# State-space stage of a ten-stage block: reordered projection, decays by matmul and by exp's bias, heads in pairs, norm per chunk

## The chip, the cores and the metric

The kernel runs on one NeuronCore of a Trainium2 chip, in one launch. The metric is the device time of that launch in microseconds. The kernel before took 2258.63 us, the median of three runs (2258.62 to 2260.26).

## The reference, cut to what matters

Two blocks of layers are computed one after the other on x of 256 tokens by 1024, in float32: ten sublayers in all. The change touches the sixth, a bidirectional state-space mixer (Mamba-2 form) with 32 heads of 64 in 8 groups with a state of 128:

```python
z, xBC, dt = split(h @ w_in)            # 2048, 4096 and 2 x 32 columns
xBC = silu(centred_conv5(xBC) + bias)   # x: 2048, B: 8 x 128, C: 8 x 128
dt  = softplus(dt + dt_bias)            # for each direction d and head
a   = cumsum(dt * -exp(a_log))          # over tokens; from the end for the backward direction
# for each head and direction:
y[t] = sum over u (u <= t, or u >= t)  exp(a[t] - a[u]) * (C[t] . B[u]) * dt[u] * x[u]
y   = (y_forward + y_backward + d_skip * x) * silu(z)
y   = rms_norm(y, over each group of 256 channels) * norm_g
out = x_res + gate * (y @ w_out)        # w_out: 2048 x 1024
```

With 256 tokens the kernel computes each head's whole 256 by 256 matrix of decays, instead of chunks with a carried state. A head's matrix has four blocks of 128 by 128 tokens. The two on the diagonal are needed in both directions, each with a triangular mask, the other two in one direction: six blocks, 768 columns.

## The kernel before

Everything is written out as one list of instructions for each engine: PE (matmuls), ACT (activations), DVE (vector operations), and SP, which issues the DMAs. Each engine runs its list strictly in order. What one engine makes and another needs is ordered by semaphore counts (`wait_ge`); nothing else plans the work, so where a helper is called decides where its instructions stand in all four queues. `vl(...)` and `al(...)` count an instruction and wait for it on its own engine.

Weights come through a ring of four slots, three chunks (1.5 MB) a DMA. Matmuls with weights use three passes in the rounded format F32R: weight and operand are each split in a high part (a copy on ACT, L559) and a low part (a subtraction on DVE, L565). `split_chunk` does that for a chunk of 128 x 1024. Matmuls on plain float32 are shown in the trace as two records each, with two passes in each.

The stage goes as follows.

- `projection` (`main`, L622 for the first two chunks together, L652 for the rest, L646 for chunks computed by tokens). For each chunk c: split chunk c+1, 24 matmuls for chunk c, then `evac(c-1)`. Chunks 0 to 15 are z, 16 to 47 the convolution's channels, 48 is dt.
- `evac` (L2169): z gets its silu (L2175). A convolution chunk is copied to a padded tile (L2187), scaled by the first tap on ACT (L2189), gets four more taps on DVE (L2197), and its silu on ACT one chunk later (`silu_out`, L2226).
- Then a chain on small tiles: exp of -|dt|, a series for log1p (L2242 to L2252), dtA, cumulative sums as matmuls with triangles of ones (L2269, L2273), the gate row (`gate_row`, L539), transposes of x (L2294) and their copies (L2300).
- The loop over heads. `group(gi)`: once for 4 heads, the product of B and C (L2323), four copies into the order of the six blocks (L2332 to L2335), and four products of x and dt (L2346). `rows(h)`: two matmuls bring a[t] to all partitions (L2363). `decays(h)`: DVE forms a[t] - a[u] plus the mask in six operations (L2377, L2379, L2380), ACT makes one exp over 768 columns (L2386). `sums(h)`: DVE multiplies by the group's product (L2396), PE makes four matmuls (L2407 to L2410) of 64 output channels; odd heads write to the upper half of the partitions. `finish(h)`, every second head: the skip term and the product with silu(z) (L2426, L2428).
- The norm: squares of all 4096 columns (L2454), sums over channels with a matmul of ones (L2468), scale, root (L2480), reciprocal over 2048 columns (L2485), 16 products (L2487).
- `out_project`: for each of 16 chunks, split the operand (L693, L698), split the weights (L559, L565), 12 matmuls of 512 columns (L709).

Of the kernel before, what the change touches and what calls it, by code (L numbers as in the profile page):

```python
# [8 lines left out]
F32R = mybir.dt.float32r  # L9
# [5 lines left out]
P = 128  # L15
# [102 lines left out]
def lay_out(i):  # L118
# [39 lines left out]
    for j in range(5):  # L158
# [33 lines left out]
        "w_ssd_in": col_chunks(padded(i["ssd_w_in_2"][0], 49 * P)),  # L192
# [31 lines left out]
def build(nc, dram, out, pat, cat):  # L224
    V, A, E = nc.vector, nc.scalar, nc.tensor
    ctx = ExitStack()
    with ctx:
# [7 lines left out]
        hT_ = sb("hT", KC * T)  # L235
        htok_ = sb("htok", NT * D)
# [7 lines left out]
        sb("slab", SLAB // 4)  # L244
        psum = ctx.enter_context(nc.psum_tensor("psum", [P, 8, 512], F32))
# [419 lines left out]
        def out_project(name, n, lhs, ready, nxt, parts_at=R_AT + 24576, wp_at=(R_AT, R_AT + 8192, R_AT + 16384)):  # L665

            parts = halves(parts_at, 4)
            wp = [chunk_parts(at) for at in wp_at]
            wp_free = [ready] * 3
            parts_free = [ready] * 4  # L670
            loads, done = [], []
# [8 lines left out]
            for k in range(n):  # L680
# [6 lines left out]
                s, full = loads[k // 3]  # L687

                @block.scalar
                def _(_e):  # L690
                    for point in parts_free[k % 4]:
                        A.wait_ge(*point)
                    Ring.p = act.count(A.activation(parts[:, 0, k % 4, :], lhs[:, k, :], ACT.Copy).then_inc(act.sem, 1))  # L693
# [6 lines left out]
                w_ready = split_chunk(slot_ap(s, SLOT)[:, (k % 3) * D:(k % 3 + 1) * D], wp[k % 3], full, wp_free[k % 3])  # L700
                Ring.used[s] = [w_ready]

                @block.tensor
                def _(_e):
                    E.wait_ge(*w_ready)
# [1438 lines left out]
        def ssd_run(h_pts, project, nxt):  # L2144
            ar = Region(W_AT + 24576)
            bc = ar.take(16 * T).rearrange("p (c t) -> p c t", t=T)
            xb_ = ar.take(16 * T)
            xb = xb_.rearrange("p (c t) -> p c t", t=T)
            zs_ = ar.take(16 * T)
            zs = zs_.rearrange("p (c t) -> p c t", t=T)  # L2150
            dt, dtA, acum = (ar.take(NT * 64) for _ in range(3))
# [3 lines left out]
            ar = Region(H_AT, W_AT + 24576)  # L2155
            tmp = [ar.take(NT * 64) for _ in range(3)]
            acT = ar.take(T)
# [9 lines left out]
            cv_free = [go] * 2  # L2167

            def evac(c, b, p):  # L2169
                if c < 16:  # L2170
                    @block.scalar
                    def _(_e):
                        A.wait_ge(*p)
                        A.wait_ge(*pad_ready)
                        Ring.q = act.count(A.activation(zs[:, c, :], b[:, 0:T], ACT.Silu).then_inc(act.sem, 1))  # L2175
                    return (Ring.q,)
                if c < 48:
                    m = c - 16
                    q = m % 2

                    @block.scalar
                    def _(_e):

                        A.wait_ge(*p)
# [18 lines left out]
                    return (freed,)  # L2203
                while pend:
                    silu_out()

                @block.vector
                def _(_e):

                    V.wait_ge(*p)  # L2210
                    bias = prm("dt_bias")
                    bb = spread(bias.rearrange("p (o n) -> p o n", o=1), [P, NT, 64])
                    vl(V.tensor_tensor(d3(dt), d3(b[:, 0:2 * 64]), bb, ALU.add).then_inc(dve.sem, 1))
                    vl(V.tensor_scalar(tmp[0], dt, -1.0, None, ALU.mult).then_inc(dve.sem, 1))
                    Ring.q = vl(V.tensor_tensor(tmp[0], tmp[0], dt, ALU.min).then_inc(dve.sem, 1))
                return (Ring.q,)

            pend, cv_silu = [], [go] * 2

            def silu_out():  # L2220
                m, q, p = pend.pop(0)

                @block.scalar
                def _(_e):
                    A.wait_ge(*p)
                    cv_silu[q] = act.count(A.activation(xb[:, m, :] if m < 16 else bc[:, m - 16, :], cv[q], ACT.Silu, bias=prm("sconv_b")[:, m:m + 1]).then_inc(act.sem, 1))  # L2226

            project(evac, h_pts)
            xt = [hT_[:, :], htok_[:, :]]
            neg_abs = Ring.q  # L2230

            @block.scalar
            def _(_e):
                A.wait_ge(*neg_abs)
                A.activation(Arow, prm("a_log"), ACT.Exp)
                Ring.q = al(A.activation(tmp[0], tmp[0], ACT.Exp).then_inc(act.sem, 1))

            @block.vector
            def _(_e):

                V.wait_ge(*Ring.q)
                vl(V.tensor_scalar(tmp[1], tmp[0], 2.0, None, ALU.add).then_inc(dve.sem, 1))  # L2242
                vl(V.reciprocal(tmp[1], tmp[1]).then_inc(dve.sem, 1))
                vl(V.tensor_tensor(tmp[0], tmp[0], tmp[1], ALU.mult).then_inc(dve.sem, 1))
                vl(V.tensor_tensor(tmp[1], tmp[0], tmp[0], ALU.mult).then_inc(dve.sem, 1))
# [531 lines left out]
```

## Time and profile before

| | |
|---|---|
| median of the runs | 2258.63 us |
| the profiled execution's own time | 2257.68 us |
| its span | 2255.9 us |
| PE busy | 2008.1 us, 89% |
| DVE busy | 1518.6 us, 67% |
| ACT busy | 1160.3 us, 51% |
| POOL busy | 0.2 us |
| mean granted clock of PE | 0.937 of full |
| DMA | 377.90 MB, 168 GB/s |

PE is the TensorE's matmuls and PEld its weight loads, DVE the VectorE, ACT the ScalarE, POOL the GpSimd. Busy is the time in which an engine has at least one instruction under way. The granted clock is 1.00 at 2.4 GHz and 0.50 at 1.2 GHz. The span goes from the first to the last instruction of the program; what lies around it (1.8 us) is part of the execution's time. The stage that the change touches goes from about 1091 to 1466 us of the span.

### The profile page before, as it was taken

Reading aid. Unit: us, or ns where it says so; the run is one execution under the profiler, and the core shown is the slowest. Engines: PE = TensorE matmul, PEld = TensorE weight load, DVE = VectorE, ACT = ScalarE, POOL = GpSimd, SP = SyncE. Lnnn points to the kernel's source line nnn. Section 1 sums busy time; section 2 is a strip of 40 time slices with the busy share of each in tenths; the row PEclk is TensorE's granted clock in tenths of the full one; section 3 lists DMA queues with packets and bytes.
Section 4 is the critical chain, followed back from the end, with each engine's and each line's share of the span. In section 5 each row is a group of like instructions: output and inputs, shape, how many; then the busy total and the mean of one; then the engine's idle time right before and its main releaser. Section 6 shows DMA issues by size and latency. Waiting matters only on the chain.

```text
span 2255.9 us, 36817 instructions
## 1 busy us (share of the span) xinstructions
PE 2008.1 (89%) x14906; PEld 1805.3 (80%) x14906; DVE 1518.6 (67%) x2429; ACT 1160.3 (51%) x2013; POOL 0.2 (0%) x4
## 2 busy tenths in 40 slices
PE   7896999898788998999999785799999997689998
PEld 6895999897568997999898553689989995368998
DVE  5667877523757777877578796687777772466554
ACT  6535665532546566665566332465565652355342
POOL 0000000000000000000000000000000000000000
PEclk9998999995889999999999898899999997789999
DMA  7203765433026664888343100468858860304551
GB/s 291 100 4 131 262 232 187 158 124 120 1 82 225 219 231 165 315 291 284 141 156 135 57 1 1 162 249 283 286 208 311 283 242 24 130 2 167 190 176 74
DMA packets 96538, 377.90 MB, mean 168 GB/s; under 512 B 5745, under 2 KB 5873, under 8 KB 95601
## 3 DMA queue, kind: packets, MB, share of 16 engines
q1 hardware_dynamic: 96368, 375.54, 46.9%
q8 instruction: 119, 1.95, 0.3%
q14 instruction: 51, 0.41, 0.1%
HBM read 374.47 MB, written 1.05 MB: 166 GB/s over the span
## 4 chain that ended last, share of the span: by engine, by line
PE 76%; DVE 18%; ACT 3%; issue 2%; DMA 0%; DVEq 0%; SPq 0%; ACTq 0%
PE psum L902 32%; PE psum L918 15%; PE psum L652 7%; PE psum L709 5%; DVE htok L2197 3%; PE psum L646 2%; DVE buf L565 2%; PE psum L1152 2%; PE psum L885 2%; PE psum L2616 1%; PE psum L494 1%; PE psum L2070 1%; DVE buf L2396 1%; PE psum L1520 1%; DVE buf L2377 1%
## 5 line engine op out<-in xcount | busy, mean ns | idle before, releaser
L902 PEld LDWEIGHTS psum<-buf,buf 128*128 128x128 f32 x6048 | 741.9, 192 | 9.3
L902 PE MATMUL psum<-buf,buf 128*128 128x256 f32 x6048 | 745.7, 283 | 0.0
L918 PE MATMUL psum<-buf,buf 128*128 128x512 f32 x1584 | 383.5, 391 | 2.2 <-DVE buf L967 2.2
L918 PEld LDWEIGHTS psum<-buf,buf 128*128 128x128 f32 x1584 | 289.2, 188 | 57.8 <-DVE buf L967 3.0
L800 DVE TENSOR_TENSOR buf<-ring,buf 128x1024 fp32r<-128x1024 f32 x264 | 311.1, 1220 | 9.5 <-DVE modT L856 7.5
L652 PE MATMUL psum<-buf,buf 128*128 128x256 f32 x2064 | 256.7, 285 | 9.2 <-DVE buf L565 9.1
L794 ACT ACTIVATE buf<-ring 128x1024 fp32r<-128x1024 f32 x264 | 263.0, 1045 | 0.0
L652 PEld LDWEIGHTS psum<-buf,buf 128*128 128x128 f32 x2064 | 249.7, 192 | 15.2 <-DVE buf L565 14.6
L565 DVE TENSOR_TENSOR buf<-ring,buf 128x1024 fp32r<-128x1024 f32 x132 | 161.2, 1224 | 129.2 <-ACT buf L559 120.3
L816 DVE TENSOR_TENSOR buf<-ring,buf 128x1024 fp32r<-128x1024 f32 x132 | 161.6, 1224 | 86.4 <-ACT buf L811 86.4
L811 ACT ACTIVATE buf<-ring 128x1024 fp32r<-128x1024 f32 x132 | 139.5, 1057 | 87.9 <-PE psum L918 85.3
L829 DVE TENSOR_TENSOR buf<-buf,crow 128x1024 f32<-128x1024 f32 x144 | 171.8, 1218 | 0.0
L559 ACT ACTIVATE buf<-ring 128x1024 fp32r<-128x1024 f32 x132 | 138.1, 1049 | 43.7 <-PE psum L709 34.4
L936 ACT ACTIVATE htok<-psum 128x256 f32<-128x256 f32 x88 | 33.8, 384 | 229.1 <-PE psum L902 229.1
L709 PE MATMUL psum<-buf,buf 128*128 128x512 f32 x480 | 118.0, 410 | 37.4 <-DVE buf L565 37.4
L840 ACT ACTIVATE buf<-buf 128x1024 f32<-128x1024 f32 x144 | 150.8, 1052 | 0.0
L963 DVE TENSOR_TENSOR htok<-htok,psum 128x256 f32<-128x256 f32 x132 | 55.3, 419 | 135.6 <-ACT htok L936 129.8
L709 PEld LDWEIGHTS psum<-buf,buf 128*128 128x128 f32 x480 | 95.7, 200 | 59.3 <-DVE buf L565 38.7
L494 PE MATMUL psum<-early,htok 128*128 128x128 f32 x160 | 41.5, 427 | 69.8 <-DVE htok L483 69.1
L494 PEld LDWEIGHTS psum<-early,htok 128*128 128x128 f32 x160 | 27.6, 203 | 84.0 <-DVE htok L483 76.7
L948 DVE SCALAR_TENSOR_TENSOR htok<-htok,params 128x256 f32<-128x256 f32 x88 | 42.7, 485 | 57.7 <-ACT htok L942 56.2
L2197 DVE SCALAR_TENSOR_TENSOR htok<-htok,params 128x256 f32<-128x256 f32 x128 | 61.9, 484 | 5.1 <-ACT htok L2189 1.3
(339 smaller groups left out, 2116.9 us busy)
## 6 DMA issues: line engine op xcount, KB each, us to landing
ring<-in_w_ffn SPq DMA_DIRECT2D x88, 1536.0 KB, 7.1
buf<-in_w_mod SPq DMA_DIRECT2D x144, 512.0 KB, 4.7
ring<-in_w_conv SPq DMA_DIRECT2D x44, 1536.0 KB, 6.6
ring<-in_w_ssd_in SPq DMA_DIRECT2D x16, 1536.0 KB, 6.4
ring<-in_w_ns_in SPq DMA_DIRECT2D x9, 1536.0 KB, 6.3
ring<-in_w_hy_in SPq DMA_DIRECT2D x7, 1536.0 KB, 19.0
ring<-in_w_ssd_out SPq DMA_DIRECT2D x5, 1536.0 KB, 6.4
ring<-in_w_cmp SPq DMA_DIRECT2D x4, 1024.0 KB, 4.8
```

Source lines behind the costliest of these rows:

```text
L559: Ring.p = act.count(A.activation(parts[:, 0, :], raw, ACT.Copy).then_inc(act.sem, 1))
L565: Ring.p = dve.count(V.tensor_tensor(parts[:, 1, :], raw, whole(parts[:, 0, :]), ALU.subtract).then_inc(dve.sem, 1))
L652: ins = E.matmul(b[:, 0:T], w[:, wa, k, :], h[:, ha, k, :], start=k + n_ == 0, stop=k == KC - 1 and n_ == 2)
L709: ins = E.matmul(acc[:, t, h * 512:(h + 1) * 512], parts[:, la, k % 4, t * P:(t + 1) * P], wp[k % 3][:, wa, h * 512:(h + 1) * 512], start= ...
L794: Ring.p = act.count(A.activation(wu[j % 2][:, 0, part], raw, ACT.Copy).then_inc(act.sem, 1))
L800: up_split[j, g] = dve.count(V.tensor_tensor(wu[j % 2][:, 1, part], raw, whole(wu[j % 2][:, 0, part]), ALU.subtract).then_inc(dve.sem, 1))
L811: Ring.p = act.count(A.activation(wd[j % 2][:, 0, :], raw, ACT.Copy).then_inc(act.sem, 1))
L816: down_split[j] = dve.count(V.tensor_tensor(wd[j % 2][:, 1, :], raw, whole(wd[j % 2][:, 0, :]), ALU.subtract).then_inc(dve.sem, 1))
L829: mod_prod[c] = dve.count(V.tensor_tensor(w, w, crow[:, :], ALU.mult).then_inc(dve.sem, 1))
L840: Ring.mod_last = act.count(A.activation(w, w, ACT.Copy, accum_out=modT[:, c:c + 1]).then_inc(act.sem, 1))
L902: ins = E.matmul(b[:, g * T:(g + 1) * T], w[:, wa, g, k, :], h[:, ha, k, :], start=k + n_ == 0, stop=k == KC - 1 and n_ == 2)
L918: ins = E.matmul(acc[:, t, g * 512:(g + 1) * 512], hr[z][:, ha, t * P:(t + 1) * P], wd[z][:, wa, g * 512:(g + 1) * 512], start=j == 0 and ...
```

## The change

The stage is rewritten from the projection to the output projection. The input weights are laid out in another order: two convolution chunks and one z chunk in turn, B and C ahead of x, and dt as chunk 2. The chain for dt, the cumulative sums, the transposes of x and the gate row are issued in `evac`, beside the projection's chunks (`beside(c)`). dt no longer multiplies x: its logarithm goes, with -a[u], into the bias of exp. The argument of exp is summed in PSUM by PE: the mask through an identity, a[t] (as high and low part, on 64 partitions) through a selection vector, both in F32R; ACT reads it from there in four operations of 256, 256, 128 and 128 columns. Sums and finish go by pairs of heads, with the two heads' matmuls in turn. The squares are made in `finish`, their sums on PE with one column, and the norm's factors are brought back to all partitions by 16 matmuls; the products with them are issued chunk by chunk inside `out_project` (`feed`). The first chunk group of the output weights is loaded behind the projection, and two of its chunks are split inside the loop. Some tiles move (acT, idr, sel into the unused end of htok; dt, bias, u1 into `small`).

```diff
+def ssd_order():
+    conv = [c for g in range(8) for c in (32 + g, 40 + g)] + list(range(16, 32))
+    out = conv[0:2] + [48]
+    for j in range(1, 14):
+        out += conv[2 * j:2 * j + 2] + [j - 1]
+    return out + conv[28:32] + [13, 14, 15]
...
-            load_a, load_b, pre_a, pre_b, project = projection("w_ssd_in", 49, h, tokens=(48,), widths={48: 64})
+            load_a, load_b, pre_a, pre_b, project = projection("w_ssd_in", 49, h, tokens=(2,), widths={2: 64})
...
+            def turn_x(n):
+                for t in range(NT):
+                        # PE
+                        E.wait_ge(*x_made[4 * n + 3])
+                        E.wait_ge(*at["t_free", t])
+                        for c in range(4):
+                            ins = E.transpose(bank(t)[:, c * P:(c + 1) * P], xb[:, 4 * n + c, t * P:(t + 1) * P], ident)
+                        # ACT
+                        at["t_free", t] = act.count(A.activation(xt[t][:, 4 * n * P:(4 * n + 4) * P], bank(t), ACT.Copy)...)
+            def beside(c):   # called at the end of evac(c)
+                if c == 3:   # DVE: waits for exp; u1 = bias + 2, reciprocal, bias *= u1, u2 = bias^2, u3 = u2 / 17
+                if c == 4:   # DVE: horner((15, 13, 11, 9)), one operation a term
+                if c == 5:   # DVE: horner((7, 5, 3)), then three operations for dt
+                if c == 6:   # DVE: dtA (4 operations), bias = max(dt, 1e-37)
+                        A.wait_ge(*at["floor"])
+                        at["log"] = al(A.activation(u1, bias, ACT.Ln).then_inc(act.sem, 1))
+                        at["back"] = act.count(A.activation(u2, u1, ACT.Exp, scale=-1.0).then_inc(act.sem, 1))
+                if c == 7:   # PE: waits for dtA; 6 matmuls of 64 columns into bank(0). DVE: two operations on u2, u1
+                if c == 8:   # DVE: waits for them; acum = bank(0), bias = u1 - acum
+                if c == 9:   # PE: 4 transposes of acum; ACT: acT = their high part
+                if c == 10:  # DVE: low part of acT, idr = ident, sel = ident[:, 0:32] + ident[:, 32:64]
+                if c == 12:
+                    at["row"] = gate_row(mod_col(0, 1, 2), 1.0, 2, [h_pts[-1]])
+                if c in (31, 37, 43, 47):
+                    turn_x((31, 37, 43, 47).index(c))
...
+            def group(gi):   # PE: two matmuls; ACT: waits for them and, from gi = 2, for g_used[gi - 2]
+                    A.activation(G_[q][:, 0:512], bank(4), ACT.Copy)
+                    ends = bank(4).rearrange("p (a n) -> p a n", a=4)[:, 0:4:3, :]
+                    g_made[gi] = act.count(A.activation(G_[q][:, 512:768]..., ends, ACT.Copy)...)
+            def rows(h):     # PE: waits for x_free[h - 2]
+                    E.matmul(X[q][:, 0:512], idr, masks[:, 0:512], start=True, stop=False)
+                    E.matmul(X[q][:, 0:512], one_head, acT[0:64, :], start=False, stop=True)
+                    E.matmul(X[q][:, 512:768], idr, masks[:, 384:640], start=True, stop=False)
+                    ins = E.matmul(X[q][:, 512:768], one_head, acT[0:64, 128:384], start=False, stop=True)
+            def exponentials(h):
+                    A.wait_ge(*at["X", h])
+                    if h >= 4:
+                        A.wait_ge(*y_summed[(h - 4) // 2])
+                    A.activation(two_of(0), x4[:, 0:4:2, :], ACT.Exp, bias=by(0, 0))
+                    A.activation(two_of(256), x4[:, 1:4:2, :], ACT.Exp, bias=by(1, 1))
+                    A.activation(e[:, 512:640], X[h % 2][:, 512:640], ACT.Exp, bias=by(0, 1))
+                    x_free[h] = act.count(A.activation(e[:, 640:768], X[h % 2][:, 640:768], ACT.Exp, bias=by(1, 0))...)
+            def products(h): # DVE: waits for x_free[h] and g_made; e *= G, 768 columns
+            def sums(c):     # PE: waits for products(2c + 1), y_free[c - 2]
+                    for n, (u, lo, w, to) in enumerate(((0, 0, 256, 0), (0, 512, 128, 0), (1, 640, 128, 128), (1, 256, 256, 0))):
+                        for o in range(2):
+                            h = 2 * c + o
+                            ins = E.matmul(y[o * HD:(o + 1) * HD, to:to + w], xt[u][:, h * HD:(h + 1) * HD],
+                                           ee[h % 4][:, lo:lo + w], start=n == 0, stop=n == 3)
+            def finish(c):   # DVE: skip term, times silu(z), square
+            def square_sums(c): # PE: two matmuls of one column
+            load_table(ACT.Exp)
+            rows(0)
+            group(0)
+            rows(1)
+            for n in range(18):
+                if n < 16:
+                    exponentials(2 * n)
+                    exponentials(2 * n + 1)
+                if n < 15:
+                    rows(2 * n + 2)
+                if 1 <= n <= 16:
+                    sums(n - 1)
+                if n < 15:
+                    rows(2 * n + 3)
+                if n % 2 and n < 15:
+                    group(n // 2 + 1)
+                if n < 16:
+                    products(2 * n)
+                    products(2 * n + 1)
+                if n >= 2:
+                    square_sums(n - 2)
+                if 1 <= n <= 16:
+                    finish(n - 1)
+                if n == 12:
+                    split_out(0, [projected])
+                if n == 14:
+                    split_out(1, [y_free[7]])
+            load_table(ACT.Sqrt)
+            # DVE: waits for the last square sums, reduce to 16 values, scale; ACT: root; DVE: reciprocal
+                for gi in range(8):   # PE
+                    for t in range(NT):
+                        ins = E.matmul(bank(4 + gi // 2)[:, gi % 2 * T + t * P:gi % 2 * T + (t + 1) * P],
+                                       spread(rs[:, 8 * t + gi:8 * t + gi + 1], [P, P]), ident, start=True, stop=True)
+            def feed(k):     # called in out_project ahead of chunk k; DVE: x times gain times factor, chunks k and k + 1
+                norm(k)
+                norm(k + 1)
+                return normed[k]
```

## Rows read from the trace of the kernel before

**Rows 1.** Windows: stretch, length; busy PE, PEld, DVE, ACT, POOL; granted clock, DMA share, GB/s.
```profile
1091.80:1249.70 157.90, 148.74 (x1185) 143.26 (x1183) 117.39 (x183) 92.37 (x161) 0.00 (x0) 1.00 0.40 144
1249.70:1271.40 21.70, 14.16 (x79) 11.77 (x77) 9.23 (x32) 7.38 (x13) 0.00 (x0) 0.69 0.22 73
1271.40:1381.40 110.00, 89.05 (x413) 56.82 (x412) 101.46 (x284) 34.88 (x64) 0.00 (x0) 1.00 0.00 1
1381.40:1421.20 39.80, 8.74 (x32) 7.12 (x32) 24.31 (x24) 9.46 (x8) 0.00 (x0) 0.68 0.00 0
1421.20:1466.40 45.20, 45.17 (x188) 37.16 (x189) 27.91 (x37) 22.76 (x33) 0.00 (x0) 0.94 0.55 203
```

**Rows 2.** Timeline in the projection's z part: start, length, engine, line, tiles, count.
```profile
1136.81 11.44 PE L652 MATMUL psum<-buf,buf 128*128 128x256 f32 x94
```

**Rows 3.** Timeline in the projection's convolution part.
```profile
1161.80 1.23 DVE L565 TENSOR_TENSOR buf<-ring,buf 128x1024 fp32r<-128x1024 f32 x1 [0.30 <-DVE htok L2197]
1162.94 2.04 DVE L2197 SCALAR_TENSOR_TENSOR htok<-htok,params 128x256 f32<-128x256 f32 x4
1163.08 3.13 PE L652 MATMUL psum<-buf,buf 128*128 128x256 f32 x24 [0.34 <-DVE buf L565]
1166.56 3.14 PE L652 MATMUL psum<-buf,buf 128*128 128x256 f32 x24 [0.36 <-DVE buf L565]
```

**Rows 4.** PE groups by form: the dt chunk's matmuls.
```profile
L646 PE MATMUL psum<-ring,hT 128*128 128x64 f32 x32 | 3.7, 273 | 0.0
```

**Rows 5.** Timeline behind the projection: the chain for dt.
```profile
1250.20 1.28 ACT L2235 ACT_TABLE_LOAD   x1
1250.46 0.29 DVE L2215 TENSOR_TENSOR buf<-buf,buf 128x128 f32<-128x128 f32 x1
1251.50 0.26 ACT L2235 ACTIVATE buf<-params 128x64 f32<-128x64 f32 x1
1252.25 0.95 DVE L2243 RECIPROCAL buf<-buf 128x128 f32<-128x128 f32 x1
```

**Rows 6.** Group by line in the loop: count, busy, mean ns, idle before.
```profile
L2396 DVE TENSOR_TENSOR buf<-buf,buf 128x768 f32<-128x768 f32 x32 | 30.5, 952 | 0.3 <-DVE buf L2428 0.3
```

**Rows 7.** Timeline in the loop over heads.
```profile
1283.05 0.48 DVE L2426 SCALAR_TENSOR_TENSOR buf<-buf,params,psum 128x256 f32<-128x256 f32 x1
1283.56 0.42 DVE L2428 TENSOR_TENSOR buf<-buf,buf 128x256 f32<-128x256 f32 x1
1284.32 0.38 PE L2410 MATMUL psum<-buf,buf 128*64 128x128 f32 x2
1284.64 1.13 PE L2363 MATMUL psum<-buf,early 64*128 64x256 f32 x4
```

**Rows 8.** Two PE groups of the first stage that alternate between halves of the array.
```profile
66.56 1.97 PE L1338 MATMUL psum<-early,small 128*64 128x128 f32 x32
L1511 PE MATMUL psum<-buf,buf 64*64 64x64 f32 x128 | 3.8, 221 | 0.0
```

**Rows 9.** ACT timelines: two operations with a bias from PSUM; one without.
```profile
34.20 0.84 ACT L1255 ACTIVATE buf<-psum,params 128x256 f32<-128x256 f32 x2 [0.19 <-PE psum L1248]
...
1271.94 0.28 ACT L2334 ACTIVATE buf<-psum 128x128 f32<-128x128 f32 x1
```

**Rows 10.** Chain of waits after the stage: start, length, engine, line, count.
```profile
1483.14 1.78 PE psum L539 x16
1490.68 2.75 PE psum L918 x12
```

**Rows 11.** Timeline of the norm.
```profile
1382.39 3.62 ACT L2454 ACTIVATE buf<-buf 128x4096 f32<-128x4096 f32 x1 [4.68 <-DVE buf L2428]
1386.06 8.74 PE L2468 MATMUL psum<-buf,buf 128*128 128x256 f32 x32 [4.68 <-ACT buf L2454]
1399.11 12.95 DVE L2485 RECIPROCAL htok<-htok 128x2048 f32<-128x2048 f32 x1 [1.98 <-ACT htok L2480]
```

**Rows 12.** Window at the start of the output projection, columns as in rows 1.
```profile
1422.00:1426.00 4.00, 4.00 (x11) 3.12 (x10) 2.45 (x4) 0.73 (x2) 0.00 (x0) 0.50 0.22 35
```

More of the change, by code:

```diff
@@ new lines, in evac, with _ @@
+            def evac(c, b, p):
+                o = order[c]
+                if o < 16:
+                    while c > 45 and pend:
+                        silu_out()
+                    @block.scalar
+                    def _(_e):
+                        A.wait_ge(*p)
+                        Ring.q = act.count(A.activation(zs[:, o, :], b[:, 0:T], ACT.Silu).then_inc(act.sem, 1))
+                    freed = Ring.q
+                elif o < 48:
+                    m = o - 16
+                    q = len(x_made) + len(pend) & 1
@@ new lines, in evac, with split_out @@
+                beside(c)
+                return (freed,)
+            project(evac, h_pts)
+            projected = (pe.sem, pe.n)
+            z_made = (act.sem, act.n)
+            row_point = at["row"]
+            wp_at = (H_AT + 8192, R_AT + 24576, R_AT)
+            wp = [chunk_parts(a) for a in wp_at]
+            out_load = load(dram["w_ssd_out"][0:3], 3)
+            out_split = {}
+            def split_out(k, free):
+                s, full = out_load
+                out_split[k] = split_chunk(slot_ap(s, SLOT)[:, k * D:(k + 1) * D], wp[k], full, free)
+                Ring.used[s] = [out_split[k]]
@@ L2238, in _ @@
+            ar = Region(W_AT, W_AT + 24576)
+            masks = ar.take(5 * P, F32R)
+            G_ = [ar.take(768) for _ in range(2)]
+            ee = [ar.take(768) for _ in range(4)]
+            sq = [ar.take(T) for _ in range(2)]
+            rs = small[:, 192:208]
             @block.vector
             def _(_e):
-                V.wait_ge(*Ring.q)
-                vl(V.tensor_scalar(tmp[1], tmp[0], 2.0, None, ALU.add).then_inc(dve.sem, 1))
-                vl(V.reciprocal(tmp[1], tmp[1]).then_inc(dve.sem, 1))
@@ L2313, in group @@
+                V.memset(whole(masks[:, P:3 * P]), 0.0)
+                for a, name in ((0, "neg_f"), (3, "neg_b"), (4, "neg_f")):
+                    ins = V.tensor_copy(masks[:, a * P:(a + 1) * P], cst(name))
+                at["masks"] = dve.count(ins.then_inc(dve.sem, 1))
+            X = [banks(2 * q, 2) for q in range(2)]
+            x_free, e_free, e_made, m_made = {}, {}, {}, {}
+            g_made, g_used, y_summed, y_free, sq_made, sq_free = {}, {}, {}, {}, {}, {}
             def group(gi):
@@ L2430, in ssd_run @@
-            group(0)
-            rows(0)
-            for h in range(34):
-                if h + 1 < 32:
-                    rows(h + 1)
-                if h < 32:
-                    decays(h)
-                if h % 4 == 1 and h // 4 + 1 < 8:
-                    group(h // 4 + 1)
-                if 1 <= h <= 32:
-                    sums(h - 1)
-                if h >= 2:
-                    finish(h - 2)
-            y_done = [(dve.sem, dve.n), (pe.sem, pe.n)]
-            sq = zs_
-            inv = htok_[:, :]
```

444 lines of the change are left out of this document (218 added, 226 removed).

## Prediction

> **What bounds the kernel now.** I read the busy totals first, then five windows over the state-space stage, then their timelines. PE is busy 89% of the span, but not in this stage. [rows 1] cut it into projection (157.9 us), a chain for dt (21.7), the loop over 32 heads (110.0), the norm (39.8) and the output projection (45.2). The reader is to see which engine fills each: PE in the first and last; nobody in the second and fourth, at a granted clock of 0.69 and 0.68; DVE, 101.5 of 110, in the loop. The change touches the first four: 329.4 us from the first matmul (1091.8) to the first of the output projection (1421.2).
>
> Within the projection a z chunk costs its 24 matmuls, 24 x 0.12 = 2.88 us [rows 2]. A convolution chunk costs 3.48 from 1163.08 to 1166.56 [rows 3]: DVE's subtraction, four taps (2.04) and 0.3 of gaps, for which PE waits 0.34. So 16 chunks are bound by PE, 32 by DVE.
>
> **Projection.** The new order has two convolutions and one z in three chunks. DVE needs 2 x 3.48 + about 1.3 = 8.3 us, PE 3 x 2.88 = 8.64: PE is the bound, by a little. PE's floor is 6.0 for the first pair, 46 x 2.88 = 132.5, and 32 x 0.115 = 3.7 for dt [rows 4]: 142.2. Into it move six matmuls for the cumulative sums (12 records, 1.4), four transposes (0.5), the gate row (1.8, L539 in [rows 10]) and 24 of 32 transposes of x (2.6): 6.3. Before, the gate row lay under DVE's chain.
>
> The dt chain is no longer alone, but it stands in DVE's queue between taps and subtractions, and PE waits for subtractions. Counted from the end of chunks 0 and 1: DVE starts at 0.9, has six convolutions' taps (6 x 2.35 = 14.1), the subtractions of chunks 3 to 10 (8 x 1.23 = 9.8), 24 small operations at 0.32 (a 0.29 operation and its wait, [rows 5]) and 0.65 more for the reciprocal (8.3). It also stands still about 3.1 us while ACT makes Exp and, later, Ln and Exp, behind which ACT's copy of the next weights is queued. So chunk 10 starts at 36.3; with PE alone it would be 3.7 + 7 x 2.88 + 1.4 = 25.3. Loss 11.0. Later, transposes of x and the gate row make ACT wait for PE before its next copy: about 0.5 a time, four times, 1.9. Projection: 142.2 + 6.3 + 11.0 + 1.9 = 161.4, so 3.5 more than before. Bounds: 149 if queues absorb it all, 168 if the ACT stalls double. If DVE's 0.3 us of slack in three chunks is not there, the later 38 chunks add up to 4 of this.
>
> ACT switches tables Silu to Exp, to Silu, to Ln and Exp, to Silu here. The row shows a switch at 1.28, the next operation 0.02 after it, and the load under way at 1250.20, before DVE made its operation's input at 1250.46 to 1250.75 [rows 5]: it runs ahead of the wait; I count it only where ACT returns to Silu. The Trainium skill, "ScalarE: Activation LUTs", "What ACT_TABLE_LOAD costs", gives about 2.66 us a switch, of which 1.38 is a drain. By that figure four switches would add 5.5 us to the total; the trace here shows no drain, so I leave it out.
>
> **From the projection's end to a running loop.** 21.7 us of chain go. Late next is ACT's last silu and turn of x (2.1 us after the end), then rows(0), the first group's product and its copies (5.3), exponentials of heads 0 and 1 and rows(2), rows(3): the steady loop starts 9.2 after the end. DVE's masks (1 us) lie under this.
>
> **The loop.** Removed from DVE: six subtractions a head and the 32 products with dt (12 us). Its new work for two heads is two products of 0.95 and three finishing operations (0.48, 0.42, 0.42 and waits): 3.3 us [rows 6, 7]. ACT: an operation on 256 columns from PSUM with a bias is 0.47, the next starts 0.36 after it two take 0.84 [rows 9]; one on 128 without a bias is 0.28, with it I take 0.37, spacing 0.25. A head is 0.36 + 0.36 + 0.25 + 0.37 = 1.33 (bounds 1.2 and 1.6); two heads 2.5, and every second pair two copies for the group, 0.8.
>
> PE: one pass over 512 columns in the rounded format is 2.75/12 = 0.229, over 256 it is 0.12 [rows 10, 2]. Rows of a head are two of each, 0.70. A change between K=128 and K=64, or to M=64, costs 0.09: L2363 starts 0.20 after the last record of L2410, whose usual spacing is 0.11 [rows 7]. Four changes make rows 1.07. Sums: 768 columns in plain f32 took 1.28 us a head (4 x 768 / 2.4 GHz; spacing 0.11 for 128 columns bears that out). Interleaved, two heads write to different halves of the array. L1338 does just that, with one moving operand for both halves: its 32 records of 128 columns take 1.97, 0.055 each and not 0.11 [rows 8]. L1511 alternates halves with operands of their own: 128 records of 64 columns take 3.8, 0.03 each, where two passes over 64 columns are 0.053 [rows 8]. So two heads cost 1.28 + 0.1 = 1.4. A group's product is 0.95 (one in two pairs), square sums 0.53. A pair is 2 x 1.07 + 1.4 + 0.5 + 0.53 = 4.5: above ACT and DVE. PE becomes the bound.
>
> But the order of ACT's queue adds a wait. The group's copies stand ahead of the next pair's exponentials, and wait for a product that PE makes last in the iteration. Over two iterations, from a start a: rows 1.07, sums to 2.45, rows to 3.5, product 4.5 and 0.17 until it has landed, copies, exponentials from 5.5 to 6.85, rows (waiting since 5.1) to 7.95, sums to 9.35, landed 9.55, exponentials to 10.9, next start at 10.95. Two pairs take 10.95, not 9.0. Seven such cycles hold 14 pairs; the last sums end 9.2 + 6 x 10.95 + 14.4 = 89.3 after the projection's end. Splitting the first output weights (1.05 ACT, 1.23 DVE, twice) falls in even iterations, where ACT is done at 7.8 and waits until 9.55: hidden; without that cover 1 us each. Per head: 2.7 us against 3.44.
>
> **Norm.** Gone are the squares (3.6), the sums over 4096 columns (8.7), a root over 2048 columns, the reciprocal (12.95) and most of the 16 products [rows 11]. Left in line: finish 1.45, square sums 0.6, reduce and scale 0.5, root 0.4, reciprocal of 16 values 0.3, then PE's 16 broadcast matmuls, 32 x 0.11 = 3.5, ahead of the output projection in its queue. The first norm products and the split of x lie under these. 6.75, and 1.0 because PE has paused and may be granted half the clock for a part: 97.1 after the projection's end. The table load of Sqrt is hidden, as it is now. The remaining norm products (0.48 a chunk) join 1.65 of DVE in chunks of 2.75: hidden, until DVE is over 2.75.
>
> **Output projection.** Before, its first four microseconds ran at 0.50 [rows 12], after 18 us without a matmul. The pause is now below 4: I take 1.6 us off (0 to 2.4). Weight DMAs are issued well ahead as before, on SP, which waits for slots only; none is added.
>
> **Sum.** 161.4 + 97.1 = 258.5 for 329.4: 70.9 less, and 1.6: 72.5. The profiled execution took 2257.68 us (span 2255.9 and 1.8 around it), 1 us under the median of 2258.63. 2257.7 - 72.5 = 2185.2, so 2186 as a median.
>
> **Rivals.**
> - Loop runs at PE's 4.5 a pair, because ACT gets through sooner (or matmuls of K=64 and K=128 follow without 0.09): 7 x 2 less, 2172. For: ACT's rows leave no doubt that it is under 3.4 us a pair; against: its queue is in order. 15%.
> - The halves don't overlap: no row has two streams of 128 partitions and 256 columns at once (L1338 shares one, L1511's have 64 partitions). 1.28 more a pair, 20 in all, 2206. Against: both rows as far as they go. 8%.
> - A full drain at each change of form. The row has L2363 at 1284.64 while L2410 lasts until 1284.70, so there was none in this case [rows 7]. If there were, 0.07 more at 11 changes in 16 pairs is 12 us: 2198. The Trainium skill, "TensorEngine Tiling (Array Packing)", "Key Properties", says that a change of tiling mode drains the TensorE; the trace speaks against a whole drain. 7%.
> - The early projection is the bound: ACT's returns to Silu and DVE's small operations delay PE by 10 more. For: DVE has only 0.3 us to spare in three chunks, so that a delay is not worked off. 2196. 17%.
> - Slower: PE, which waits in every cycle, is granted half its clock from the loop on. PE's parts of a cycle double: 17.7 instead of 10.95, 47 more over the loop, 10 at its ends, and 41 in the output projection if the clock stays down through it: 2284. It decides once over 73 us come together, that is the whole loop and a third of the output projection at half clock. Against: now PE idles 20 us of the loop and has 1.00 [rows 1]. 3%.
>
> **How the numbers follow.** Forecast 50%, its own range 2178 to 2194. The range of 8 in 10 takes in the first rival and the second: 2166 to 2208. 0.2% (4.5 us) is what can be told from no change. Everything but the slow rival is faster: 95%; same 2%, slower 3%, a little more than its own case for mishaps.
>
> **What would show it.** Projection about 161 us with PE gaps in chunks 5 to 10 and hardly any afterwards; PE's first row of the loop 3 us behind it; L-lines of sums in pairs that start within 0.01 us; ACT waiting for the group's product, some 2 us every second pair; period 10 to 11 us; norm below 10 us; DVE below 70% in the loop. Wrong would be: sums spaced at 0.21, a granted clock below 0.95 in the loop, or a projection over 170.

## The result and the profile after

The changed kernel took 2234.30 us, the median of four runs (2232.84 to 2235.93); the kernel before took 2258.62 beside it. The ratio is 0.9893, with an interval from 0.9881 to 0.9905: 24 us faster, a third of the 72.5 forecast, and outside the range of 2166 to 2208. The profiled execution took 2232.84 us, its span is 2231.1 us.

The page of the kernel after, busy time:

```profile
PE 2023.7 (91%) x14962; PEld 1811.3 (81%) x14962; DVE 1452.3 (65%) x2226; ACT 1175.9 (53%) x2102; POOL 0.2 (0%) x4
```

PE is busy for 15.6 us longer than before although the kernel is faster, and DVE 66 us less. The windows of the stage after, with the columns of [rows 1]: projection, loop, norm, and the output projection with 1.3 us behind it.

```profile
1090.60:1256.40 165.80, 156.18 (x1244) 153.28 (x1243) 126.58 (x214) 104.78 (x179) 0.00 (x0) 0.97 0.42 149
1256.40:1390.40 134.00, 119.03 (x481) 68.41 (x479) 53.07 (x83) 54.87 (x153) 0.00 (x0) 0.69 0.02 9
1390.40:1397.10 6.70, 4.70 (x40) 4.54 (x41) 4.25 (x12) 1.60 (x5) 0.00 (x0) 1.00 0.00 0
1397.10:1440.90 43.80, 43.80 (x195) 35.94 (x193) 32.61 (x48) 22.23 (x32) 0.00 (x0) 1.00 0.59 210
```

The reader is to see the second line. The chain for dt [rows 1] is gone as a stretch of its own, and of the four that are left, the norm and the output projection came out about as forecast and the projection is 4.4 us too long. The loop, 134.0 us with its start, was forecast at 89.3. PE is busy 119 us of it, at a granted clock of 0.69; DVE and ACT are at 40%.

The chain of waits after, from the last sums (L2488) through the norm to the end of the output projection (L727):

```profile
1388.86 1.55 PE psum L2488 x16
...
1393.52 3.84 PE psum L2566 x32
1397.36 42.23 PE psum L727 x186
```

The whole norm takes 7.0 us where before it took 39.8, 12.95 of them in one reciprocal [rows 1, 11]. The last sums of the loop, at the full clock again, take 1.55.

From the first matmul of the projection to the end of the output projection the stage takes 349.0 us; the forecast has 302.1 (374.6 less 72.5). The 46.9 between them, in the forecast's own terms:

| | forecast | measured | difference |
|---|---|---|---|
| projection | 161.4 | 165.8 | +4.4 |
| end of the projection to the last sums | 89.3 | 134.0 | +44.7 |
| norm | 7.75 | 7.0 | -0.8 |
| output projection | 43.6 | 42.2 | -1.4 |

Outside the stage, its start is 1.2 earlier and what follows it is 2.0 longer, which the forecast left alone and no run looked into.

PE's timeline after, over one cycle of two pairs in the loop (rows L2438 to L2441, sums L2488, group product L2412):

```profile
1311.50 0.80 PE L2438 MATMUL psum<-buf,buf 128*128 128x512 f32 x1 [1.56 <-ACT buf L2461]
...
1313.97 1.55 PE L2488 MATMUL psum<-buf,hT 128*64 128x256 f32 x8
1315.30 1.49 PE L2488 MATMUL psum<-buf,buf 128*64 128x128 f32 x8
...
1318.66 0.48 PE L2438 MATMUL psum<-buf,buf 128*128 128x512 f32 x1
1319.07 0.49 PE L2439 MATMUL psum<-buf,buf 64*128 64x512 f32 x1
1319.49 0.39 PE L2440 MATMUL psum<-buf,buf 128*128 128x256 f32 x1
1319.81 0.38 PE L2441 MATMUL psum<-buf,buf 64*128 64x256 f32 x1
1320.12 1.55 PE L2488 MATMUL psum<-buf,hT 128*64 128x256 f32 x8
1321.46 1.49 PE L2488 MATMUL psum<-buf,buf 128*64 128x128 f32 x8
...
1324.65 1.13 PE L2412 MATMUL psum<-buf 128*128 128x256 f32 x4
...
1327.99 0.79 PE L2438 MATMUL psum<-buf,buf 128*128 128x512 f32 x1 [1.87 <-ACT buf L2461]
```

The cycle is 16.5 us, 1311.50 to 1327.99, where 10.95 was forecast. It is the shortest of six: from one wait to the next they take 16.5 to 18.0 us, 17.1 on average. There are two new things in it. First, a head's rows take 1.46 even at the full clock, 1318.66 to 1320.12, not 1.07. Second, most of the cycle isn't at the full clock. Windows of the same cycle:

```profile
1311.50:1314.00 2.50, 2.50 (x6) 1.18 (x6) 1.90 (x2) 1.20 (x4) 0.00 (x0) 0.50 0.00 0
1314.00:1316.70 2.70, 2.70 (x17) 1.58 (x16) 0.00 (x0) 0.00 (x0) 0.00 (x0) 0.50 0.00 0
1316.70:1318.60 1.90, 1.90 (x10) 1.15 (x8) 1.64 (x4) 1.66 (x5) 0.00 (x0) 1.00 0.00 0
...
1320.10:1322.90 2.80, 2.80 (x18) 1.64 (x17) 0.55 (x1) 0.00 (x0) 0.00 (x0) 0.50 0.00 0
```

The clock is at 1.2 GHz behind the wait, at 2.4 from 1316.7 (rows of a head at the full clock follow, 1318.66 on), and back at 1.2 at 1320.1, with no idle time on PE ahead of this second fall. The sums of a pair take 2.83 us at half clock. Why this one cycle goes back to the full clock between them, no run looked into.

ACT's timeline after shows the wait that the forecast had put into the cycle, its copy of the group's product:

```profile
1309.33 0.60 ACT L2421 ACTIVATE buf<-psum 128x512 f32<-128x512 f32 x1 [7.29 <-PE psum L2412]
```

### The profile page after: what moved, and what is told of

The parts are those of the page before. It is cut to its first block, busy times and chain, and to the rows that moved or that the text cites. A ratio compares the mean times of both kernels' runs of the same rounds, so it can differ in the third digit from the quotient of the medians.

```text
span 2231.1 us, 36837 instructions
## 1 busy us (share of the span) xinstructions
PE 2023.7 (91%) x14962; PEld 1811.3 (81%) x14962; DVE 1452.3 (65%) x2226; ACT 1175.9 (53%) x2102; POOL 0.2 (0%) x4
## 4 chain that ended last, share of the span: by engine, by line
PE 83%; DVE 11%; ACT 4%; issue 2%; DMA 0%; DVEq 0%; SPq 0%; ACTq 0%
PE psum L920 32%; PE psum L936 15%; PE psum L662 9%; PE psum L727 5%; PE psum L656 2%; PE psum L2488 2%; PE psum L1170 2%; PE psum L903 2%; PE psum L2713 1%; PE psum L504 1%; PE psum L2088 1%; DVE buf L575 1%; PE psum L1538 1%; PE psum L1143 1%; DVE buf L1089 1%
## 5 line engine op out<-in xcount | busy, mean ns | idle before, releaser
L727 PE MATMUL psum<-buf,buf 128*128 128x512 f32 x480 | 115.4, 403 | 11.4 <-DVE buf L575 11.4
L727 PEld LDWEIGHTS psum<-buf,buf 128*128 128x128 f32 x480 | 93.8, 196 | 32.2 <-DVE buf L575 12.2
```

Source lines behind the costliest of these rows:

```text
L727: ins = E.matmul(acc[:, t, h * 512:(h + 1) * 512], parts[:, la, k % 4, t * P:(t + 1) * P], wp[k % 3][:, wa, h * 512:(h + 1) * 512], start= ...
```

## The experiments

All kernels do the whole computation. The theories of the first four runs: (A) PE falls to half clock because its matmuls fill too little of the loop's time; (B) the pairwise sums, alternating between the array's halves, lower the clock by their form; (C) the wait for ACT alone does it. From e5 on there are two more, about the time of a head's rows: (D) changes between operands of 128 and 64 partitions (K=128 and K=64) cost more than forecast; (E) the cost lies elsewhere. A loop time below is that of its window, from the projection's end to the last sums, in a profiled run. The kernel before had medians of 2259.11, 2259.99 and 2259.76 us beside the three sets (e1 to e4, e5 to e8, e9 to e11).

### e1: the sums head by head

```diff
-                    for n, (u, lo, w, to) in enumerate(...):
-                        for o in range(2):
+                    for o in range(2):
+                        for n, (u, lo, w, to) in enumerate(...):
```

> The changed kernel, but the sums of a pair run head by head (the loop over heads outside the loop over blocks), so that its matmuls no longer alternate between the halves of the array. Theory A (share: the clock is halved because the array streams for too small a share of the loop, since interleaving halves the time of the sums and the waits for ACT stay): streaming goes up by 1.3 us a pair, the granted clock of the loop from 0.68 to 0.95 or more, sums of a pair again about 2.7 us, a cycle of two pairs 13.6 instead of 16.5, about 2216 us. Theory B (form: matmuls in halves are not counted as activity): also 0.95 or more and about 2216. Theory C (the wait for the group's copies alone makes the clock fall): that wait is still there, the clock stays near 0.68, the sums take up to 5 us, 2250 or more.

Measured: 2238.19 us, ratio 0.9906 (0.9891 to 0.9920). Window of its loop:

```profile
1257.90:1393.90 136.00, 120.57 (x482) 77.46 (x480) 53.05 (x83) 54.75 (x153) 0.00 (x0) 0.81 0.02 10
```

The sums get longer, the loop stays about as long, and the clock is higher, 0.81 and not 0.69, but not full. None of the three theories had this: A and B had 0.95 or more and 2216 us, C had 0.68 and 2250 or more. Pairing does not slow the kernel, but whether it lowers the clock this run can't say: longer sums also fill PE's time otherwise.

### e2: the group's product at the head of the iteration

```diff
             for n in range(18):
+                if n % 2 and n < 15:
+                    group(n // 2 + 1)
                 if n < 16:
...
-                if n % 2 and n < 15:
-                    group(n // 2 + 1)
```

> The changed kernel, but PE makes the group's product at the head of the iteration, ahead of rows(2n+2), instead of at its end, so that ACT does not wait for it ahead of the next exponentials. [...] Theory B (form): the clock stays near 0.68, PE is busy nearly all the time at half clock, 2225 to 2235. Theory C (the wait alone): 1.00, about 2182.

Measured: 2205.45 us, ratio 0.9765 (0.9751 to 0.9780). Window of its loop:

```profile
1256.90:1360.70 103.80, 101.39 (x481) 59.27 (x480) 53.15 (x83) 56.29 (x153) 0.00 (x0) 0.82 0.03 13
```

The wait is gone: PE idles 2.4 us of the loop, not 15. That accounts for 12.6 of the 30.2 us; the rest is in the busy time, which goes with the clock of 0.82. So the time is not B's (2225 or more), and without the wait the clock is still not full, so C is not the whole of it. The clock also moves inside this loop: its window from 1297 to 1317 has 1.00, with cycles of 10.6 us, and the one from 1337 to 1360 has 0.61, though PE idles only 0.4 us in it.

### e3: eight matmuls more in every pair

```diff
+                    for _i in range(8):
+                        E.matmul(bank(7)[:, 256:512], idr, masks[:, 0:256], start=True, stop=True)
...
+                if n < 16:
+                    fill()
```

> The changed kernel with eight more matmuls of 256 columns in the rounded format (idr times masks into an unused part of bank 7, read by nobody) behind each pair's square sums, where PE waits for ACT: 0.86 us more of work a pair at full clock. Theory A (share): the granted clock of the loop rises to 0.95 or more, although the work is more, a cycle of two pairs falls from 16.5 to about 12, 2200 to 2208. Theory B (form): the windows of the sums stay at half clock; 2232 to 2255, the filler costs or is hidden. Theory C (the wait alone, which the filler covers): as A.

Measured: 2217.73 us, ratio 0.9817 (0.9802 to 0.9831): 16.6 us faster than the kernel after, by work that nobody reads. Window of its loop, and its timeline at a pair's sums (L2488) beside the added matmuls (L2519):

```profile
1257.90:1373.50 115.60, 107.98 (x609) 70.54 (x607) 53.15 (x83) 54.75 (x153) 0.00 (x0) 0.94 0.03 11
```

```profile
1313.66 1.19 PE L2519 MATMUL psum<-buf,buf 128*128 128x256 f32 x8
...
1316.07 0.87 PE L2488 MATMUL psum<-buf,hT 128*64 128x256 f32 x8
1316.77 0.82 PE L2488 MATMUL psum<-buf,buf 128*64 128x128 f32 x8
```

128 matmuls more, and PE is busy 11 us less. The clock is about what A had, the time is 10 us above its range. The same alternating sums take 1.52 here, 1316.07 to their end at 1317.59, where they took 2.83 in the kernel after. B falls: their form is not slow, and with it in the loop the clock is 0.94 here and full in e5 and e9.

### e4: e2 with four matmuls more

```diff
+                    for _i in range(4):
+                        E.matmul(bank(7)[:, 256:512], idr, masks[:, 0:256], start=True, stop=True)
```

> Group's product early as in the run before last, and four filler matmuls a pair. Theory A (share): clock 1.00, a cycle of two pairs 9.5 to 10.5 us, about 2183 to 2190. Theory B (form): clock near 0.68, no faster than the changed kernel, 2225 to 2240. Theory C: 1.00, 2185.

Measured: 2204.57 us, ratio 0.9756 (0.9739 to 0.9772), not told apart from e2. Window of its loop:

```profile
1258.10:1363.40 105.30, 103.27 (x545) 64.05 (x543) 53.05 (x83) 56.31 (x153) 0.00 (x0) 0.89 0.03 13
```

The higher clock pays for the added matmuls and no more. C falls further: 2 us idle, and the clock still isn't full. A's forecast, 1.00 and 2183 to 2190, missed too.

### e5: e2 with all rows on 128 partitions

```diff
+                        V.memset(whole(acT[64:128, :]), 0.0)
+                        V.memset(whole(sel[64:128, :]), 0.0)
...
-                    one_head = spread(sel[0:64, h:h + 1], [64, P])
+                    one_head = spread(sel[:, h:h + 1], [P, P])
...
-                    E.matmul(X[q][:, 0:512], one_head, acT[0:64, :], start=False, stop=True)
+                    E.matmul(X[q][:, 0:512], one_head, acT[:, :], start=False, stop=True)
```

and the same for columns 512 to 768.

> Group's product early (the run at 2205.5 us), and the selection vector and a[t] are filled with zeros to 128 partitions, so that no matmul of rows has K=64. Same columns, four changes of form a head gone. Theory D (each change between K=128 and K=64 exposes a weight load, 0.2 us here instead of the forecast 0.09): rows fall from 1.46 to about 0.75, a pair from 5.3 to about 3.9, the granted clock stays at 1.00 since the share of streaming rises, loop 103 to 70 to 80 us, 2175 to 2182. Theory E (the cost is in changing between identity and selection or between accumulation groups, not in K): rows stay at 1.46, 2205.

Measured: 2173.38 us, ratio 0.9612 (0.9596 to 0.9629). Window of its loop, and PE's timeline for the rows of one head (L2440 to L2443) and what follows them:

```profile
1263.90:1334.70 70.80, 64.53 (x481) 49.00 (x479) 53.05 (x83) 53.87 (x153) 0.00 (x0) 1.00 0.05 19
```

```profile
1303.87 0.49 PE L2440 MATMUL psum<-buf,buf 128*128 128x512 f32 x1
1304.20 0.39 PE L2441 MATMUL psum<-buf,buf 128*128 128x512 f32 x1
1304.44 0.28 PE L2442 MATMUL psum<-buf,buf 128*128 128x256 f32 x1
1304.55 0.28 PE L2443 MATMUL psum<-buf,buf 128*128 128x256 f32 x1
1304.67 0.50 PE L2512 MATMUL psum<-small,buf 128*128 128x1 f32 x4
```

A head's rows take 0.80 here (1303.87 to 1304.67) and 1.46 in the kernel after: multiplying twice as many partitions, half of them zeros, saves 0.66. The pair's other head, ahead of the sums, takes 0.89 (1301.53 to 1302.42). In the kernel after the heads take 1.47 and 1.46, so like for like it is 0.67 and 0.57. D came true, a little better than forecast. The spacings are 0.33, 0.24, 0.11 and 0.12 against 0.41, 0.42, 0.32 and 0.31. PE idles more than in e2, 6.3 us of the loop, and has the full clock. (The profiled run is the slowest of e5's four, 2177.36 us: its projection took 168.0.)

### e6: e2 with the order of the rows changed

```diff
                     E.matmul(X[q][:, 0:512], idr, masks[:, 0:512], start=True, stop=False)
-                    E.matmul(X[q][:, 0:512], one_head, acT[0:64, :], start=False, stop=True)
                     E.matmul(X[q][:, 512:768], idr, masks[:, 384:640], start=True, stop=False)
+                    E.matmul(X[q][:, 0:512], one_head, acT[0:64, :], start=False, stop=True)
```

> Group's product early, and in rows both mask matmuls come first, then both with the selection vector (K=64): two changes of form a head instead of four, everything else as it was. Theory D: rows from 1.46 to about 1.25, 0.4 a pair, 6 us, about 2199. Theory E (accumulation groups change more often in this order): no gain or a loss, 2205 to 2210.

Measured: 2180.94 us, ratio 0.9643 (0.9629 to 0.9658). Window of its loop, and PE's timeline for one head:

```profile
1257.00:1333.60 76.60, 72.89 (x481) 47.17 (x479) 53.03 (x83) 54.17 (x153) 0.00 (x0) 1.00 0.04 17
```

```profile
1306.93 0.50 PE L2438 MATMUL psum<-buf,buf 128*128 128x512 f32 x1
1307.27 0.28 PE L2439 MATMUL psum<-buf,buf 128*128 128x256 f32 x1
1307.48 0.50 PE L2440 MATMUL psum<-buf,buf 64*128 64x512 f32 x1
1307.82 0.28 PE L2441 MATMUL psum<-buf,buf 64*128 64x256 f32 x1
1308.03 0.87 PE L2488 MATMUL psum<-buf,hT 128*64 128x256 f32 x8
```

Two changes instead of four: 1.10 for this head, which stands ahead of the sums, 0.21 above e5's 0.89; the other takes 1.09 (1305.35 to 1306.44), 0.29 above 0.80. So a change costs 0.10 to 0.15 here, and the two that are gone 0.18 to 0.19 each. The same instructions in another order save 24.5 us against e2. Of the 27.2 us off the loop some 12 are the shorter rows (32 x 0.37); the rest goes with the clock, 1.00 and not 0.82.

### e7 and e8: the projection

e7 is e2 with the steps for dt beside chunks 5, 8, 11, ..., 26 instead of 3 to 10. e8 is e2 with ACT's copies of turned x one `evac` later than PE's transposes.

```diff
-                if c == 3:
+                if c == 5:
```

```diff
+                if c in (32, 38, 44, 48):
+                    turn_copy((32, 38, 44, 48).index(c))
```

> Group's product early, and the eight steps of the dt chain go beside chunks 5, 8, 11, ..., 26 (the z chunks) instead of 3 to 10. Theory F (the forecast's 11 us: the steps are too dense for DVE and ACT early on, and later chunks have slack): projection from 166.6 to about 160, 2198 to 2200. Theory G (DVE has no slack to give anywhere, 0.3 us in three chunks): the loss only moves, 165 to 167, 2205.

> Group's product early, and ACT's copies of the turned x stand one evac later in its queue, so that ACT does not wait for PE ahead of its copy of the next weights. Theory H (that wait makes PE stop 1.7 us at three of the four turns, where 0.5 was forecast): projection from 166.6 to 162, 2200 to 2201. Theory I (the stop comes from the copies' own time, 1.1 us): at most 1 us.

Measured: e7 2190.66 us, ratio 0.9707 (0.9675 to 0.9738); e8 2201.30 us, ratio 0.9743 (0.9728 to 0.9758). Windows of their projections, e7 and then e8 (e2's takes 165.8):

```profile
1091.30:1254.40 163.10, 155.22 (x1244) 151.10 (x1243) 126.23 (x213) 104.74 (x178) 0.00 (x0) 0.99 0.42 152
```

```profile
1093.20:1256.80 163.60, 154.90 (x1244) 153.02 (x1243) 126.68 (x214) 104.97 (x179) 0.00 (x0) 0.97 0.42 151
```

Spreading takes 2.7 off the projection, where theory F had 6 to 7; the later copies take 2.2, about half of theory H's, and its time came true. The rest of e7's 14.8 us is not projection: its loop is 10.5 us shorter, at 0.93 instead of 0.82, with the same code. Nor is it a sure gain of the edit. Three of e7's four runs took 2189.86 to 2191.43 at a mean clock of 0.941 or 0.942, the other 2205.32 at 0.933, as e2's four do (2203.24 to 2210.68, at 0.933 or 0.934). The same kernel comes out either way by what clock it is granted; why is open.

### e9: e5's rows on 128 partitions, alone

The edit of e5 on the kernel after, with the group's product where it was.

> The changed kernel with the selection vector and a[t] on 128 partitions and nothing else: the group's product stays at the end of the iteration, so ACT's wait for it stays. Forecast's step (with PE at full clock that wait makes a cycle of two pairs about 2 us longer than the work): clock 1.00, a cycle 10 to 10.5 where it is 8.3 without the wait, loop about 86, 2188 to 2190. Rival (the wait alone brings half clock, whatever the matmuls are): clock below 0.8, a cycle of 13 or more, 2205 to 2220.

Measured: 2188.89 us, ratio 0.9693 (0.9676 to 0.9709). Window of its loop, and its timeline at the wait:

```profile
1259.80:1344.90 85.10, 65.63 (x482) 49.41 (x480) 52.97 (x83) 53.87 (x153) 0.00 (x0) 1.00 0.04 16
```

```profile
1303.45 0.60 ACT L2423 ACTIVATE buf<-psum 128x512 f32<-128x512 f32 x1 [3.01 <-PE psum L2414]
...
1305.62 0.50 PE L2440 MATMUL psum<-buf,buf 128*128 128x512 f32 x1 [1.87 <-ACT buf L2463]
```

This is the decisive run. PE's wait is 1.87, as in the kernel after, and PE idles 19.5 us of the loop, more than the 15 there; the clock is 1.00. So C is refuted: the wait by itself does not lower the clock. Beside rows of mixed form it does go with a lower one, 0.69 with the wait and 0.82 without it (e2). The cycle of two pairs takes 10.3 us, where 10.95 was forecast.

### e10 and e11: the four edits together, and pairing by itself

e10 joins e5, e7 and e8. e11 is e5 with e1's order of sums.

> All four edits that gained: group's product early, 128 partitions in rows, the steps of the dt chain beside chunks 5, 8, ..., 26, ACT's copies of the turned x one evac later. If their gains in the projection add (2.7 and 2.1 us there, loop 70): 2168 to 2170. If the two edits of the projection take away the same stops: 2171.

> The run with the group's product early and 128 partitions (2173.4 us, clock 1.00), but sums head by head, not alternating. At full clock the alternation is worth what the forecast gave it, 1.28 us a pair: pairs at 5.2 and 5.7 instead of 3.9 and 4.4, loop 90, 2193 to 2195. Rival (DVE or ACT at 3.3 to 3.9 already holds the pair, PE has room): 0.6 to 1.0 a pair, 2183 to 2189.

Measured: e10 2166.94 us, ratio 0.9591 (0.9577 to 0.9606); e11 2183.25 us, ratio 0.9665 (0.9651 to 0.9679). Windows of e10's projection and loop, then e11's loop:

```profile
1091.30:1252.70 161.40, 154.30 (x1244) 150.95 (x1243) 127.11 (x215) 104.85 (x178) 0.00 (x0) 0.99 0.42 153
1252.70:1323.30 70.60, 64.62 (x482) 49.01 (x479) 53.05 (x83) 53.97 (x153) 0.00 (x0) 1.00 0.05 19
```

```profile
1260.80:1342.00 81.20, 75.70 (x481) 58.77 (x479) 53.08 (x83) 53.87 (x153) 0.00 (x0) 1.00 0.04 15
```

e10 beats both kernels: 93 us under the one before, 67 under the one after. The two gains in the projection nearly add: 161.4 is 4.4 under e2's 165.8. With both at the full clock, alternating sums are worth 9.9 us (e5's median against e11's): a pair's sums take 1.52 in turn and 2.22 head by head. That is the size that the rival had, but not for its reason: PE has little room, it idles 5.5 us of e11's loop against 6.3 of e5's.

## Why the prediction was wrong

**Right.** The norm (7.0 against 7.75) and the output projection (42.2 against 43.6): the pause ahead of it is short, and its clock is 1.00 where it began at 0.50 [rows 12]. The halves overlap: the second rival is wrong, and its price of 1.28 a pair is 0.70 (e11), since with sums head by head the last matmuls of one head already overlap with the first of the next. ACT's wait for the group's product is there in every second pair, and costs what was forecast: e9, in which nothing else disturbs, has a cycle of 10.3 against 10.95, and without the wait 8.3 (e5: pairs of 3.9 and 4.4). The first rival thus names an edit that pays, but not what happens. DVE is at 40% in the loop.

**Projection, 4.4 too short.** The chain for dt cost about what was forecast: chunk 10 starts at about 1133.8, 37.0 behind chunks 0 and 1, where 36.3 was forecast. PE's timeline after, its two longest stops:

```profile
1113.79 4.30 PE L662 MATMUL psum<-buf,buf 128*128 128x256 f32 x24 [2.17 <-DVE buf L575]
...
1129.39 1.86 PE L662 MATMUL psum<-buf,buf 128*128 128x256 f32 x7 [2.70 <-DVE buf L575]
```

Behind each of them PE ran partly at half clock (0.68 from 1113.79 to 1118.00, 0.66 from 1129.39 to 1133.80), which the forecast's term does not have.

The turns of x and the gate row were taken at 1.9 together, and e8 takes 2.2 off by the copies of the turns alone: about right. DVE's timeline at one of the turns:

```profile
1208.05 2.45 DVE L575 TENSOR_TENSOR buf<-ring,buf 128x1024 fp32r<-128x1024 f32 x2 [1.82 <-ACT buf L569]
```

DVE waits 1.82 there, but PE has work ahead and idles 0.08 in the two microseconds from 1208. Most of the 4.4 lies right behind the chain, where the forecast had hardly any stops. From 1136.70 to 1156.24 PE has chunks 11 to 15 (14.4), four transposes (0.35) and the gate row (1.7), and takes 3.1 us more than these. The longest stop:

```profile
1144.52 3.14 PE L662 MATMUL psum<-buf,buf 128*128 128x256 f32 x24 [1.21 <-DVE buf L575]
```

The fourth rival, 10 us of delay, did not come.

**The failed step: PE at its full clock in the loop.** The sum of the loop has all its terms at the full clock; half clock is only in the fifth rival, at 3%. Measured was 0.69. From the first rows of one cycle to those of the next, the six cycles between 1266.49 and 1369.88 took 103.4 us, 17.2 each where 10.95 was forecast: 37.7 of the 44.7 us. The rest lies ahead of them (0.9) and in the last stretch (6.1). The dearer rows, below, are worth three heads' on the path of a cycle, 3 x 0.39 = 1.2 us, 7 us over six cycles, and would make it about 12.1; the other 31 us is what is left for the clock. This split is an estimate. The rival had the loss, 47 us for the loop, but put it down to waiting, and was given 3% because before PE idles 21 us of the loop and has 1.00 [rows 1]. That argument looked only at idle time. PE idles less after, 15 us, and has 0.69; e9 idles 19.5 and has 1.00; e4 idles 2 and has 0.89. What e9 and e6 take away is not idle time but changes of form, and both have the full clock. The rival's second half did not come: the output projection kept its clock, so that the kernel stayed faster.

**The mis-sized term beside it: "A change between K=128 and K=64, or to M=64, costs 0.09 ... Four changes make rows 1.07".** Rows take 1.46. Head against like head the four changes are worth 0.57 (1.46 less 0.89 in e5) and 0.67 (1.47 less 0.80), so 0.14 to 0.17 each; by e6, in which two are left, 0.10 to 0.19 each. The rows without changes are 0.80 to 0.89 and not 0.70 either. The row it was read from had part of this. L2363 starts 0.20 after the last record of L2410, whose spacing is 0.11 [rows 7]: that was counted. But its four records last 1.13, where three spacings of 0.213 (two passes over 256 columns at 2.4 GHz) and a last record of 0.376 make 1.02: another 0.10 sits behind the change, and was not counted. The third rival took 0.16 a change, by the overlap in the same row, and so had the size nearly right under the name of a full drain; it got 7%. Beside this: the Trainium skill, "TensorEngine Tiling (Array Packing)", "Key Properties", says that a change of tiling mode drains the TensorE. Here the matmul behind a change still starts about 0.07 before the end of the one ahead, 1319.49 against 1319.07 + 0.49 (an end that the profile models), and yet the change has its cost.

**What is shown and what is not.** Shown: removing the operands of 64 partitions alone takes 45 us off (e9 against after), reordering them 24.5 off e2; the wait alone isn't the cause, the alternating sums aren't either, and added matmuls raise the clock (e3, e4). So the loss goes with two things together, the rows of mixed form and the wait for ACT, and the rows are the larger part: without them the loop is 48.9 us shorter (e9), without the wait 30.2 (e2). Not shown: what exactly in them the chip reacts to. A change costs time in which PE gets less done, so theory A stays possible as a reading of e3, e5, e6 and e9, though its forecasts for e1 and e4 missed; K=64 also leaves the array half filled; and in e6, which keeps the matmuls on 64 partitions, both the time for changes and the order differ. No run added idle time or half-filled matmuls without changes. Nor is it shown that the dearer change is what set off the half clock: with changes at the forecast 0.09 the clock might have fallen as well. Why the clock differs between parts of e2's loop, and between runs of e7, is open too.

## What to carry to other kernels

When a change brings in matmuls of another form, price the change on both of its sides: the start of the new form behind the old and the length of its first record. Where PE becomes the bound of a loop with small mixed matmuls, ask what the granted clock will be and don't argue from idle time alone. Before an edit is credited with a gain in a part that it does not touch, look at the clock of every run (e7). Padding an operand with zeros to 128 partitions, or grouping matmuls of one form, can be worth more than the work they add. A wait in an in-order queue that is foreseen (here ACT's for the group's product) should be moved before the kernel is run, since e2 took 29 us off by moving two lines.

## What the runs showed of the hardware

- A change between 64 and 128 contraction partitions in the rounded format cost 0.10 to 0.19 us (after, e5, e6); the four of a head, 0.57 to 0.67.
- The granted clock fell to 0.50 in a stretch in which PE had no idle time (1320.1 to 1322.9 of the kernel after), and stayed at 1.00 in a loop with idle times of 1.87 us (e9).
- With the same instructions, one run of e7 took 2205.32 us at a mean granted clock of 0.933 and three took 2189.86 to 2191.43 at 0.941 or 0.942.
- 128 matmuls of 256 columns added to the loop made the kernel 16.6 us faster (e3).
- Ln and Exp, one right behind the other, took a table load each. ACT's timeline after:

```profile
1119.47 1.28 ACT L2259 ACT_TABLE_LOAD   x1
...
1125.20 0.31 ACT L2259 ACTIVATE small<-small 128x128 f32<-128x128 f32 x1 [4.45 <-DVE small L2254]
1125.53 1.28 ACT L2260 ACT_TABLE_LOAD   x1
```

The first load ends 4.45 us ahead of the operation that waits; the second stands between Ln and Exp.
